# The second normalisation of a mixture-of-experts trunk: its passes shared among VectorE, ScalarE and GpSimd

## The chip, the core and the metric
One core of a Trainium2 chip runs the whole program. The metric is the device time of one execution in microseconds (us); lower is better. The core has five instruction streams that matter here: TensorE (PE), VectorE (DVE), ScalarE (ACT), GpSimd (POOL) and SyncE (SP), which issues transfers. They meet only through semaphores: an instruction increments one when it is done, and another engine waits for a count.

## The reference, cut to what matters
The program is one step of a trunk with 1088 tokens (1024 of a prompt, 64 of a running stream) of 1024 features. The last thing it computes is the second layer normalisation, on all tokens:

```python
def layer_norm(x, g, b):
    mu = jnp.mean(xf, -1, keepdims=True)
    var = jnp.mean(jnp.square(xf - mu), -1, keepdims=True)
    return ((xf - mu) * lax.rsqrt(var + LN_EPS) * g + b)
...
    x = layer_norm(ALPHA * x + jnp.einsum('bte,ed->btd', merged, w_out), ln1_g, ln1_b)   # h2
    ffn = routed_experts(h2, idx, wts, w_eg, w_eu, w_ed) + shared
    x = layer_norm(ALPHA * x + ffn, ln2_g, ln2_b)        # the second normalisation
```

Everything is float32. The reference has ahead of it a mixer (stick-breaking attention and a recurrence) and a router with 64 experts, of which each token uses 8.

## The kernel before, in words
`build` runs the mixer, a bridge (first normalisation, router, shared expert), the loop over 64 experts, `overflow` (skipped at run time when no expert overflows), and last `combine`, which holds the second normalisation. Only `combine` is touched. Each part is a `Phase`: a block of instructions for each engine with its own semaphores, and a barrier of all engines at its end, so nothing of `combine` starts before the experts are through.

The expert loop's sums lie in device memory (`ys_d`). The residual rows `xr`, the gain `gcol` and the shift `bcol` (the last two the same on all 128 partitions) were loaded to SBUF near the end of the expert loop (L2047 to L2049). `combine` works on nine tiles `t` of 128 tokens by 1024 features; the last has 64 tokens (`rows(t)`). SP issues all nine loads of `ys` at once (L2485), then, for each tile in order, waits for `y_ready` and stores the tile (L2490). For each tile the engines do this:

- DVE, `add` (L2498): y = ALPHA * xr + y, one pass over 1024 columns, with the row sum as accumulator.
- ACT: the mean from the sum (L2528, one column), then (y - mean) squared with its row sum (L2530, one pass), then the root of the variance (L2532, one column).
- DVE, `finish`: z = (y - mean) * gain (L2505, one pass, written over `xr`), the reciprocal of the root (L2508, one column), and y = z * reciprocal + shift (L2511, one pass).

DVE's written order is `add(0)`, `add(1)`, `finish(0)`, `add(2)`, `finish(1)` and so on to `finish(8)`: an `add` runs one tile ahead. The order is written out by hand; an engine does its instructions strictly in that order, and waits at the first whose semaphore isn't there. GpSimd has no instruction in `combine`. PE has none either.

`scalar_tensor_tensor` takes two tensors and one value for each partition: (in0 op0 scalar) op1 in1. In all three passes of DVE both tensors lie in SBUF.

Of the kernel before, what the change touches and what calls it, by code (L numbers as in the profile page):

```python
# [16 lines left out]
ACT = mybir.ActivationFunctionType  # L17
ALU = mybir.AluOpType
# [7 lines left out]
NT = (T + P - 1) // P  # L26
# [32 lines left out]
def rows(t):  # L59
    return P if t < NT - 1 else T - P * (NT - 1)  # L60
# [79 lines left out]
def build(nc, a, o):  # L140

    ctx = ExitStack()
    with ctx:
# [61 lines left out]
        overflow(nc, a, ps, ident, h2_d, ys_d, tok_d, plan_d, gates_d, only_d, dest_d, picks_d, pairs_d, step_d, limit_d, bufs)  # L205
        c2.close()
        combine(nc, o, ys_d, *ahead)


# [2256 lines left out]
def combine(nc, o, ys_d, gcol, bcol, xr):  # L2466


    with ExitStack() as c:
        ys = c.enter_context(nc.sbuf_tensor("ysr", [P, NT, D], F32))  # L2470
        total, mean, spread, root, inverse = (c.enter_context(nc.sbuf_tensor(n, [P, NT], F32))
                                              for n in ("total2", "mean2", "spread2", "root2", "inverse2"))
        sq = c.enter_context(nc.sbuf_tensor("sq2", [P, 2, D], F32))
        eps = c.enter_context(nc.sbuf_tensor("eps2", [P, 1], F32))
        with Phase(nc, "x_in0 x_in1 x_in2 x_in3 x_in4 x_in5 x_in6 x_in7 x_in8 eps_set summed centre spread_ready root_ready inverted "
                       "gained y_ready stored") as (block, (
                x_in0, x_in1, x_in2, x_in3, x_in4, x_in5, x_in6, x_in7, x_in8, eps_set, summed, centre, spread_ready, root_ready,
                inverted, gained, y_ready, stored)):
            x_in = (x_in0, x_in1, x_in2, x_in3, x_in4, x_in5, x_in6, x_in7, x_in8)

            @block.sync  # L2481
            def _(sp):
                for t in range(NT):
                    m = rows(t)
                    sp.dma_start(ys[:m, t, :], ys_d[t * P:t * P + m, :]).then_inc(x_in[t], 16)  # L2485
                for t in range(NT):
                    m = rows(t)
                    sp.wait_ge(y_ready, t + 1)
                    dst = o[0][0, t * P:t * P + m, :] if t < NT - 1 else o[1][0, :, :]
                    sp.dma_start(dst, ys[:m, t, :]).then_inc(stored, 16)  # L2490
                sp.wait_ge(stored, 16 * NT)

            @block.vector
            def _(dve):
                def add(t):
                    m = rows(t)
                    dve.wait_ge(x_in[t], 16)
                    dve.scalar_tensor_tensor(out=ys[:m, t, :], in0=xr[:m, t, :], scalar=ALPHA, in1=ys[:m, t, :], op0=ALU.mult, op1=ALU.add,  # L2498
                                             accum_out=total[:m, t:t + 1]).then_inc(summed, 1)

                def finish(t):
                    m = rows(t)
                    y, z = ys[:m, t, :], xr[:m, t, :]
                    dve.wait_ge(centre, t + 1)
                    dve.scalar_tensor_tensor(out=z, in0=y, scalar=mean[:m, t:t + 1], in1=gcol[:m, :], op0=ALU.add,  # L2505
                                             op1=ALU.mult).then_inc(gained, 1)
                    dve.wait_ge(root_ready, t + 1)
                    dve.reciprocal(inverse[:m, t:t + 1], root[:m, t:t + 1]).then_inc(inverted, 1)  # L2508
                    dve.wait_ge(inverted, t + 1)
                    dve.wait_ge(gained, t + 1)  # L2510
                    dve.scalar_tensor_tensor(out=y, in0=z, scalar=inverse[:m, t:t + 1], in1=bcol[:m, :], op0=ALU.mult,  # L2511
                                             op1=ALU.add).then_inc(y_ready, 1)

                dve.memset(eps[:, :], LN_EPS).then_inc(eps_set, 1)
                for t in range(NT):
                    add(t)
                    if t >= 1:
                        finish(t - 1)
                finish(NT - 1)

            @block.scalar
            def _(act):
                act.wait_ge(eps_set, 1)
                for t in range(NT):
                    m = rows(t)
                    col = slice(t, t + 1)
                    act.wait_ge(summed, t + 1)
                    act.activation(mean[:m, col], total[:m, col], ACT.Copy, scale=-1.0 / D).then_inc(centre, 1)  # L2528
                    act.wait_ge(centre, t + 1)
                    act.activation(sq[:m, t % 2, :], ys[:m, t, :], ACT.Square, bias=mean[:m, col], accum_out=spread[:m, col]).then_inc(spread_ready, 1)  # L2530
                    act.wait_ge(spread_ready, t + 1)
                    act.activation(root[:m, col], spread[:m, col], ACT.Sqrt, scale=1.0 / D, bias=eps[:m, :]).then_inc(root_ready, 1)  # L2532

# [25 lines left out]
```

## Time and profile before

| | |
|---|---|
| time, median of 3 runs | 2656.3 us (2650.55 to 2661.9) |
| the profiled execution | 2651.97 us, span 2650.3 us |
| busy over the span | PE 92%, PEld 82%, DVE 73%, ACT 52%, POOL 51% |
| `combine`, 2607.0 to 2650.3 us | 43.3 us, of which DVE busy 33.5, ACT 16.8, POOL 0 and PE 0 |

A row of the timeline gives an instruction's start in us from the span's start, its duration in us, its engine and line, its operation, what it writes and reads with partitions x elements, and in square brackets the time that the engine sat idle before it and what ended that. A duration counts from the point where the engine takes the instruction up: an instruction that is taken up and then held shows a long duration, not an idle time. A run of instructions on one engine overlaps by some hundredths of a us, so the distance from start to start is a little less than the duration. A row of the groups gives line, engine, operation, names, shapes and count, then busy us in total, mean ns of one, and the idle time before them.

### The profile page before, as it was taken

The page shows a single profiled execution, that of the slowest core. Times are in us where ns is not written, and L with a number is a line of the kernel's source. Part 1 is how long each engine was busy: PE and PEld are TensorE (multiplying, and loading weights), DVE is VectorE, ACT ScalarE, POOL GpSimd, SP SyncE. Part 2 cuts the span into 40 slices and gives each one's busy share as a digit, 9 for nine tenths or more (in the row PEclk, how much of TensorE's full clock was granted, in tenths as well). Part 3 has the DMA queues.
Part 4 walks back from the last instruction along what each step waited for, and adds up shares of the span by engine and source line. Part 5 has one row for each costly group of instructions (what it writes and reads, how often), then busy time and mean ns, then how long its engine had stood idle before and what let it go on. Part 6 is the DMA issues. An engine that isn't in the chain of part 4 may idle for free. (4 is left out here: it accounts for less than half of the span.)

```text
span 2650.3 us, 40161 instructions
## 1 busy us (share of the span) xinstructions
PE 2431.2 (92%) x14824; PEld 2183.7 (82%) x14824; DVE 1923.1 (73%) x3073; ACT 1373.6 (52%) x2032; POOL 1339.5 (51%) x1317
## 2 busy tenths in 40 slices
PE   4999999999999999999986999699999999999990
PEld 4889898898998989989875775499989898888980
DVE  7475765757758567575676687578888888888875
ACT  3443625426245263452633332267777777777772
POOL 6354664646546556455564265334555455554320
PEclk9999999999999999999987999799999999999995
DMA  5201111111110111101113323489999999999994
GB/s 183 61 26 33 54 34 45 34 40 46 42 45 28 39 45 39 57 25 41 45 73 115 102 75 134 119 261 285 311 305 310 302 303 311 307 313 313 352 333 162
DMA packets 207582, 380.77 MB, mean 144 GB/s; under 512 B 22694, under 2 KB 129546, under 8 KB 206874
## 3 DMA queue, kind: packets, MB, share of 16 engines
q1 hardware_dynamic: 180330, 302.31, 33.0%
q0 software_dynamic: 25824, 71.42, 11.8%
q10 hardware_dynamic: 1232, 4.46, 0.4%
q8 instruction: 119, 1.95, 0.3%
q14 instruction: 77, 0.63, 0.1%
HBM read 314.84 MB, written 72.97 MB: 146 GB/s over the span
## 5 line engine op out<-in xcount | busy, mean ns | idle before, releaser
L122 PE MATMUL ps<-xTh,w_mix_low 128*128 128x368 f32 (+1 forms) x1728 | 595.8, 345 | 10.2 <-POOL w_mix_low L116 8.8
L123 PE MATMUL ps<-xTl,w_mix_high 128*128 128x368 f32 (+1 forms) x1728 | 569.6, 330 | 0.0
L124 PE MATMUL ps<-xTh,w_mix_high 128*128 128x368 f32 (+1 forms) x1728 | 567.5, 328 | 0.0
L2087 POOL DMA_INDIRECT ys_d<-yo,tab_early x114 | 214.2, 1879 | 426.9 <-DVE yo L2259 263.9
L122 PEld LDWEIGHTS ps<-xTh,w_mix_low 128*128 128x128 f32 x1728 | 326.0, 189 | 21.9 <-issue 18.6
L123 PEld LDWEIGHTS ps<-xTl,w_mix_high 128*128 128x128 f32 x1728 | 326.2, 189 | 9.1 <-issue 6.2
L124 PEld LDWEIGHTS ps<-xTh,w_mix_high 128*128 128x128 f32 x1728 | 325.6, 188 | 0.0
L2129 PE MATMUL ps<-xghl,wgh 128*128 128x320 f32 (+5 forms) x1024 | 271.4, 347 | 13.5 <-DVE xghl L116 6.9
L2129 PE MATMUL ps<-xghl,wuh 128*128 128x320 f32 (+5 forms) x1024 | 263.4, 344 | 0.0
L2131 PE MATMUL ps<-xghl,wgl 128*128 128x160 f32 (+5 forms) x1024 | 240.0, 234 | 0.0
L2131 PE MATMUL ps<-xghl,wul 128*128 128x160 f32 (+5 forms) x1024 | 238.6, 233 | 0.0
L1275 POOL TENSOR_TENSOR x_m<-x_m,kh_m 128x128 f32<-128x128 f32 (+1 forms) x272 | 126.8, 466 | 218.0 <-ACT x_m L828 218.0
L116 POOL TENSOR_TENSOR w_mix_low<-w_mix_raw,w_mix_high 128x1024 fp32r<-128x1024 f32 x72 | 174.6, 2426 | 88.5 <-ACT w_mix_high L111 88.2
L2129 PEld LDWEIGHTS ps<-xghl,wgh 128*128 128x128 f32 x1024 | 194.3, 190 | 28.6 <-ACT yo L2201 13.8
L2131 PEld LDWEIGHTS ps<-xghl,wgl 128*128 128x128 f32 x1024 | 198.0, 193 | 1.2
L2131 PEld LDWEIGHTS ps<-xghl,wul 128*128 128x128 f32 x1024 | 196.3, 192 | 0.0
L116 DVE TENSOR_TENSOR wdl<-wd_early,wdh 128x2048 fp32r<-128x2048 f32 x64 | 146.8, 2294 | 64.4 <-ACT wdh L111 64.4
L2129 PEld LDWEIGHTS ps<-xghl,wuh 128*128 128x128 f32 x1024 | 192.4, 188 | 0.0
L2075 POOL DMA_INDIRECT xg_early<-h_d,tab_early x72 | 168.9, 2346 | 42.2 <-issue 21.4
L116 DVE TENSOR_TENSOR wul<-wu_early,wuh 128x2048 fp32r<-128x2048 f32 x64 | 146.7, 2292 | 37.7 <-ACT wuh L111 37.7
L1255 POOL CAST sph_m<-l_m 128x128 fp32r<-128x128 f32 (+3 forms) x112 | 60.0, 536 | 203.1 <-PE ps L596 142.2
L2201 ACT ACTIVATE yo<-ps,wcol 128x512 f32<-128x512 f32 x228 | 143.9, 680 | 10.7 <-issue 5.3
(378 smaller groups left out, 5968.8 us busy)
## 6 DMA issues: line engine op xcount, KB each, us to landing
wd_early<-in_w_exp_down SPq DMA_DIRECT2D x64, 1024.0 KB, 9.2
wg_early<-in_w_exp_gate SPq DMA_DIRECT2D x124, 512.0 KB, 7.5
wu_early<-in_w_exp_up SPq DMA_DIRECT2D x124, 512.0 KB, 5.8
w_mix_raw<-in_w_in SPq DMA_DIRECT2D x72, 512.0 KB, 3.9
mT_d<-gs_m SPq DMA_DIRECT2D x8, 544.0 KB, 2.7
xr_m<-in_x_prompt SPq DMA_DIRECT2D x8, 512.0 KB, 3.7
xn_d<-xr_m SPq DMA_DIRECT2D x8, 512.0 KB, 2.8
out<-vrow_m SPq DMA_DIRECT2D x8, 512.0 KB, 4.8
```

Source lines behind the costliest of these rows:

```text
L116: return dve.tensor_tensor(lo, x, hi.bitcast(F32), ALU.subtract)
L122: pe.matmul(out, ll, rh, start=start, stop=False)
L123: pe.matmul(out, lh, rl, start=False, stop=False)
L124: return pe.matmul(out, lh, rh, start=False, stop=stop)
L1255: pool.tensor_copy(high, l[:kr, s, 0:wd]).then_inc(hi_done, 1)
L1275: pool.tensor_tensor(xs, xs, seg(q, LEVELS[i], side), ALU.mult).then_inc(x_done, 1)
L2075: pool.indirect_dma_start(out=xg[:m, b, j, :], out_offset=None, in_=h2_d[:, :], in_offset=rows_of(e, j, m), bounds_check=last_row, oob_is_ ...
L2087: pool.indirect_dma_start(out=ys_d[:, :], out_offset=rows_of(e, j, m), in_=yo[:m, b, j, :], in_offset=None, compute_op=ALU.add, bounds_che ...
L2129: pe.matmul(ps[:, bank + f, 0:2 * cap], wh[:, k, cols], xhl[:, k, 0:2 * cap], start=k == 0, stop=False, skip_group_check=True)
L2131: mm = pe.matmul(ps[:, bank + f, 0:cap], wl[:, k, cols], xhl[:, k, 0:cap], start=False, stop=k == KT - 1, skip_group_check=True)
L2201: act.activation(yo[:m, b, j, q * 512:(q + 1) * 512], ps[part, DB[n], :], ACT.Copy, scale=wcol[part, b, j:j + 1]).then_inc(y_ready, 1)
```

## The change
It touches `combine` alone.

- ACT gets a pass more: it writes xr = y - mean (`Identity` with the mean as bias, signalled by the new semaphore `centred`), and then squares that instead of y - mean.
- DVE's `finish` becomes `scale`: the reciprocal, and one pass, y = xr * reciprocal * gain. The centring pass is gone from it. `scale` runs two tiles behind `add`, not one.
- GpSimd gets a pass: y = y + shift, after which the tile is signalled as ready for its store.

```diff
-                def finish(t):
+                def scale(t):
                     m = rows(t)
-                    y, z = ys[:m, t, :], xr[:m, t, :]
-                    dve.wait_ge(centre, t + 1)
-                    dve.scalar_tensor_tensor(out=z, in0=y, scalar=mean[:m, t:t + 1], in1=gcol[:m, :], op0=ALU.add,
-                                             op1=ALU.mult).then_inc(gained, 1)
                     dve.wait_ge(root_ready, t + 1)
                     dve.reciprocal(inverse[:m, t:t + 1], root[:m, t:t + 1]).then_inc(inverted, 1)
                     dve.wait_ge(inverted, t + 1)
-                    dve.wait_ge(gained, t + 1)
-                    dve.scalar_tensor_tensor(out=y, in0=z, scalar=inverse[:m, t:t + 1], in1=bcol[:m, :], op0=ALU.mult,
-                                             op1=ALU.add).then_inc(y_ready, 1)
+                    dve.wait_ge(centred, t + 1)
+                    dve.scalar_tensor_tensor(out=ys[:m, t, :], in0=xr[:m, t, :], scalar=inverse[:m, t:t + 1], in1=gcol[:m, :],
+                                             op0=ALU.mult, op1=ALU.mult).then_inc(gained, 1)
...
                 for t in range(NT):
                     add(t)
-                    if t >= 1:
-                        finish(t - 1)
-                finish(NT - 1)
+                    if t >= 2:
+                        scale(t - 2)
+                scale(NT - 2)
+                scale(NT - 1)
+
+            @block.gpsimd
+            def _(pool):
+                for t in range(NT):
+                    m = rows(t)
+                    pool.wait_ge(gained, t + 1)
+                    pool.tensor_tensor(ys[:m, t, :], ys[:m, t, :], bcol[:m, :], ALU.add).then_inc(y_ready, 1)
...
                     act.wait_ge(centre, t + 1)
-                    act.activation(sq[:m, t % 2, :], ys[:m, t, :], ACT.Square, bias=mean[:m, col], accum_out=spread[:m, col]).then_inc(spread_ready, 1)
+                    act.activation(xr[:m, t, :], ys[:m, t, :], ACT.Identity, bias=mean[:m, col]).then_inc(centred, 1)
+                    act.wait_ge(centred, t + 1)
+                    act.activation(sq[:m, t % 2, :], xr[:m, t, :], ACT.Square, accum_out=spread[:m, col]).then_inc(spread_ready, 1)
```

## Rows read from the trace of the kernel before
**Rows 1.** Busy time by stage: us, then each engine's busy us and count, clock, DMA share, GB/s.

```profile
2607.00:2650.30 43.30, 0.00 (x0) 0.00 (x0) 33.51 (x46) 16.81 (x37) 0.00 (x0) 0.50 0.55 206
```

**Rows 2.** The chain that ended last, parts of it: start us, us, what.

```profile
2618.67 1.20 DVE xr L2505
2619.87 0.09 DVE inverse L2508
...
2619.98 1.28 DVE ysr L2511
2621.26 1.14 DVE ysr L2498 x2
2622.40 1.20 DVE xr L2505
...
2644.97 1.28 DVE ysr L2511
```

**Rows 3.** Timeline of SP: the last store of the program.

```profile
2646.27 0.51 SPq L2490 DMA_DIRECT2D out<-ysr  x1
```

**Rows 4.** Timeline of ACT and DVE at the first tiles of `combine`.

```profile
2612.26 0.20 ACT L2528 ACTIVATE mean<-total 128x1 f32<-128x1 f32 x1 [19.84 <-DVE ysr L2498]
2612.50 1.15 ACT L2530 ACTIVATE sq<-ysr,mean 128x1024 f32<-128x1024 f32 x1
...
2613.76 1.28 ACT L2532 ACT_TABLE_LOAD   x1
...
2615.05 0.29 ACT L2532 ACTIVATE root<-spread,eps 128x1 f32<-128x1 f32 x1
2615.25 0.19 ACT L2528 ACTIVATE mean<-total 128x1 f32<-128x1 f32 x1
...
2616.04 0.15 DVE L2508 RECIPROCAL inverse<-root 128x1 f32<-128x1 f32 x1
2616.24 1.28 DVE L2511 SCALAR_TENSOR_TENSOR ysr<-xr,inverse,bcol 128x1024 f32<-128x1024 f32 x1
```

**Rows 5.** ScalarE's lines L887 (Identity) and L883 (Sqrt), alternating: min/median/max ns.

```profile
L887 ACT ACTIVATE xr_m<-xr_m,st x9: 1240/1242/1247, 9.3 to 53.8; 128x1024 f32<-128x1024 f32 x8, 64x1024 f32<-64x1024 f32 x1
...
L883 ACT ACT_TABLE_LOAD  x1: 1283/1283/1283, 3.1 to 3.1; - x1
```

**Rows 6.** GpSimd's timeline near the start: two-input passes over 1024 columns.

```profile
21.02 2.34 POOL L116 TENSOR_TENSOR w_mix_low<-w_mix_raw,w_mix_high 128x1024 fp32r<-128x1024 f32 x1
23.31 3.32 POOL L1311 TENSOR_TENSOR xr_m<-xr_m,b_in_m 128x1024 f32<-128x1024 f32 x1
```

**Rows 7.** GpSimd's timeline at the end of the bridge.

```profile
1595.52 0.97 POOL L1902 DMA_INDIRECT tok_d<-pairs,dest  x1 [0.30 <-issue]
1614.66 2.34 POOL L1894 TENSOR_TENSOR y<-y,bcol 64x1024 f32<-64x1024 f32 x1 [18.17 <-DVE y L1632]
```

**Rows 8.** VectorE's timeline in the stretch of rows 6, and a little later.

```profile
21.20 3.23 DVE L1157 TENSOR_TENSOR xr_m<-xr_m,g_in_m 128x1024 f32<-128x1024 f32 x1
...
24.55 2.10 DVE L1149 SCALAR_TENSOR_TENSOR st<-st 128x1 f32<-128x1 f32 x1
...
33.61 0.16 DVE L1149 SCALAR_TENSOR_TENSOR st<-st 128x1 f32<-128x1 f32 x1
...
36.94 1.22 DVE L1157 TENSOR_TENSOR xr_m<-xr_m,g_in_m 128x1024 f32<-128x1024 f32 x1
```

**Rows 9.** Timelines near 191 us: GpSimd, and a VectorE pass that reads PSUM.

```profile
191.17 2.34 POOL L116 TENSOR_TENSOR w_mix_low<-w_mix_raw,w_mix_high 128x1024 fp32r<-128x1024 f32 x1
...
191.95 1.23 DVE L1088 TENSOR_TENSOR pm_m<-ps,masks 128x1024 f32<-128x1024 f32 x1 [1.24 <-PE ps L654]
```

**Rows 10.** The load of tile 2, issued at 2607.9: count, KB, us to landing.

```profile
ysr<-ys_d SPq DMA_DIRECT2D x1, 512.0 KB, 7.1
```

**Rows 11.** Timelines near 1461 us: VectorE's pass, then GpSimd's that waited for it.

```profile
1460.24 1.23 DVE L1632 TENSOR_TENSOR y<-y,gcol 128x1024 f32<-128x1024 f32 x1
...
1461.64 2.36 POOL L1894 TENSOR_TENSOR y<-y,bcol 128x1024 f32<-128x1024 f32 x1 [13.06 <-DVE y L1632]
```

More of the change, by code:

```diff
@@ L2475, in combine @@
         with Phase(nc, "x_in0 x_in1 x_in2 x_in3 x_in4 x_in5 x_in6 x_in7 x_in8 eps_set summed centre spread_ready root_ready inverted "
-                       "gained y_ready stored") as (block, (
+                       "gained y_ready stored centred") as (block, (
                 x_in0, x_in1, x_in2, x_in3, x_in4, x_in5, x_in6, x_in7, x_in8, eps_set, summed, centre, spread_ready, root_ready,
-                inverted, gained, y_ready, stored)):
+                inverted, gained, y_ready, stored, centred)):
             x_in = (x_in0, x_in1, x_in2, x_in3, x_in4, x_in5, x_in6, x_in7, x_in8)
```

## The prediction
> **What bounds the kernel now.** I looked first for where the touched code stands in the span. The table of busy time by stage shows the last 43.3 us of a span of 2650.3 as a stage by itself: PE and GpSimd do nothing in it, DVE is busy for 33.5 us and ACT for 16.8 [rows 1]. All that comes before is untouched and ends in a barrier, so the change can only move these 43.3 us, 1.6% of the program. The shares of the whole page (PE 92%) say nothing here.
>
> Then the chain that ended last. Once the first loads are in, it never leaves DVE: 1.14 for the add, 1.20 for the centring, 0.11 for the reciprocal and the wait behind it (2619.87 to 2619.98), 1.28 for the last pass, then the next tile [rows 2]. From one centring to the next it is 2622.40 - 2618.67 = 3.73 us a tile, with ACT's work and the stores beside it. The last pass starts at 2644.97 and ends at 2646.25; SP issues its store at 2646.27 [rows 3], and the span ends 4.05 us after that pass. So DVE bounds the stage now, at three passes a tile.
>
> **The change part by part.** *DVE.* The centring pass goes: 9 x 1.20 = 10.8 us off DVE's own work. What stays for a tile is add 1.14 + reciprocal and wait 0.11 + scale 1.20 = 2.45 us; the product takes the place of a sum in the last pass, at the same shape and with the same two SBUF tensors, so I give it the same duration.
>
> *ACT.* For a tile it now has the mean 0.24 (2612.26 to 2612.50), the centring, the squares with their accumulator 1.26 (2612.50 to 2613.76) and the root 0.20 to 0.31 (2615.05 to the next mean at 2615.25, or to its own end and a wait) [rows 4]. The added pass isn't in this stage's trace. The nearest rows are the squares with a bias, 1.15, and the Identity passes of the first normalisation, which have a scale too, 1.24 [rows 5]; they are its two ends, and I take 1.15, since the new pass has a bias alone, and 0.04 for the wait behind it: 1.19. ACT comes to 3.0 us a tile, still under 3.73. The wait for `centred` inside ACT holds only the squares of the same tile.
>
> *GpSimd.* Nine two-input passes over 1024 columns. The trace has this very form: 2.34 alone, also for 64 partitions [rows 6, 7], from start to start 2.29 (21.02 to 23.31). I count 2.31 between neighbours.
>
> If the three engines worked side by side, ACT would bound the stage at 3.0. But the trace shows that GpSimd's pass and a DVE pass on two SBUF tensors do not overlap. At 21.20 DVE takes up a product of two SBUF tensors while GpSimd is in a pass from 21.02 to 23.36; the product takes 3.23 us and ends at 24.43, where the same line takes 1.22 undisturbed [rows 6, 8]. It stood still until 23.2 and then ran in full. GpSimd's next pass is taken up at 23.31, while DVE's has the way, and lasts 3.32 instead of 2.34: it in turn began at 24.3, as DVE ended. DVE's `scalar_tensor_tensor` on a single column, 0.16 us elsewhere, then takes 2.10 and ends at 26.65, with GpSimd's end at 26.63 [rows 6, 8]. And a DVE pass that takes one tensor from PSUM ran 1.23 us in the middle of a GpSimd pass of 2.34, both undisturbed [rows 9]. So the pair is exclusive, for whole instructions and in both directions, when DVE reads two tensors from SBUF; `add` and `scale` both do.
>
> The Trainium skill says the same in SBUF — State Buffer, "SBUF: two separate sides": VectorE and GpSimd share a port pair under an exclusive lock, which a two-SBUF-input instruction of VectorE needs against a GpSimd one that reads SBUF, and the loser blocks for the whole instruction. Its next section, "A bandwidth-pool intuition that's wrong (but worth ruling out)", says of one such case that the loser goes on about 115 ns after the winner's end. The rows above show no such gap: by that figure, an estimate, the 14 handovers counted below would bring 1.6 us over the sum without gaps.
>
> So the exclusive work of a tile becomes add 1.14 + GpSimd 2.31 + scale 1.20 = 4.65 us, in place of 3.73. *The order of it.* GpSimd's pass t waits for `scale(t)`; when that ends, DVE's next `add` has been waiting in line and goes first. Then DVE does a reciprocal and waits for its semaphore, and GpSimd has the way; the next `scale` is held until it is through, and behind `scale` in DVE's line stand the `add` of a later tile and so ACT's mean of it. ACT has two to three tiles of lead, so this costs no more than the lock itself.
>
> *The start.* The loads are as before. `scale(0)` needs `root(0)`: before it ended at 2615.34, now 1.19 later, 2616.53; the reciprocal and its wait take 0.20 (2616.04 to 2616.24) [rows 4], so `scale(0)` starts at 2616.75. Ahead of it in DVE's line stands `add(2)`, whose load was issued at about 2607.8 and landed 7.1 us later, 2614.9 [rows 10]: done by 2616.1, hidden. The table load of 1.28 ahead of the first root stays [rows 4].
>
> *The sum.* From 2616.75: `scale(0)` 1.20; six rounds of `add`, GpSimd, `scale` (adds 3 to 8), 6 x 4.65 = 27.9; then there is no `add` left, and GpSimd 6, `scale(7)`, GpSimd 7, `scale(8)`, GpSimd 8 follow one another, where GpSimd starts each time 0.17 us after DVE's signal, as it did behind DVE's pass of 1460.24 to 1461.47 [rows 11]: 3 x 2.31 + 3 x 0.17 + 2 x 1.20 + 0.03 = 9.9. With `scale(0)` that is 39.0, and ends at 2655.7, against 2646.25 before: +9.5 us. The observed pair was a little tighter: from 21.02 to 26.63, GpSimd, DVE and GpSimd took 5.61 where pitches of 2.31, 1.15 and 2.35 give 5.81, 0.1 less for each handover. With 14 of them (two in each round, two in the tail) the sum falls by 1.4, to +8.1. I take +8.5, nearer to the pair that was seen. The tail behind the last pass stays at 4.05 us: the store is the same, and stores come 4.5 us apart instead of 3.7.
>
> The profiled execution took 2651.97, so the changed one should take 2660.5. The median of the runs shown is 4.3 higher, 2656.3; I set the prediction on it: 2656.3 + 8.5 = 2664.8.
>
> **The rivals.** (1) *The engines overlap*, because what was seen at 21 us has another cause, or GpSimd's adds fall into DVE's gaps. Then ACT bounds the stage: `root(0)` at 2616.53, eight more tiles at 3.0 us, `root(8)` at 2640.5; then 0.2 + 1.28 for `scale(8)`, 0.17 + 2.34 for the shift, ending at 2644.5, 1.8 us before the 2646.25 of now. Time 2654.5. It is the one case that is not slower. It decides from the point where DVE is held for less than 3.73 - 2.45 = 1.28 us of GpSimd's 2.31 in a tile. For it speaks that the exclusion was read in one stretch alone, and that a GpSimd pass and a DVE pass do overlap where one operand is in PSUM [rows 9]; against it speak all three waits of rows 6 and 8.
>
> (2) *ACT swaps tables for every tile*, if Identity and Sqrt don't stand in one. Two loads of 1.28 would make ACT 5.6 us a tile: eight tiles 44.8 behind 2616.53, then 1.5, 2.5 and 4.05: span 2669.4, +19 us, 2675.4. Against it: in the first normalisation Identity and Sqrt alternate nine times behind a single load [rows 5].
>
> (3) *GpSimd's first pass comes late*, since all it did for the last thousand us was to issue indirect transfers. In the bridge its two-input pass came behind a series of these and took 2.34 with no delay other than its wait for DVE [rows 7]. The Trainium skill (GPSIMD Engine Reference, "2.1 Instruction dispatch") gives some 6 us for the first call of freshly loaded code, which does not show in the profile. Worked out from rows, as a late start of one whole GpSimd pass and its round, 4.65 us behind `scale(0)`, the time would be 2669.5, as the lock would stand idle meanwhile.
>
> **How the numbers follow.** The forecast (alternation under the lock) gets 85%, rival 1 8%, rival 2 2%, rival 3 3%, and 2% are left for what I don't see. The forecast's own bounds are +8.1 and +9.5, with ACT's 1.24 instead of 1.15 lost behind the lock; more comes from the spread of the executions, 2650.55 to 2661.9, which moves a median of a few runs by 3 to 4 us. The range is 2656 to 2671: it holds nearly all of the forecast and rival 3, and leaves out most of rivals 1 and 2. Half a per cent, about what a measurement of this kernel can tell from no change, is 13.3 us. The forecast's 8.5 lies inside it, so most of its 85% is "same"; a share of some 14% of it, by the spread, and rivals 2 and 3 in part make "slower" 0.17; faster by so much would need a third of the stage to vanish, 0.02.
>
> **What would show it.** Right: in `combine`, DVE's `scale` passes with durations near 3.3 us (1.2 + most of 2.3) and no idle time named for them, GpSimd's passes near 3.4 where an `add` is ahead of them, one tile every 4.5 to 4.65 us, ACT idle for a third of the time, and the last GpSimd pass 4 us before the end. DVE's busy time in the stage would rise although it lost a pass. Wrong: `scale` at 1.28 and a tile every 3.0 us (rival 1), more than one table load (rival 2), or a gap between the first `scale` and the first GpSimd pass (rival 3). The forecast fails as a number if stages ahead of 2607 move too.

## The result and the profile after
The changed kernel takes 2663.02 us (median of 15 runs, 2656.51 to 2668.04) against 2653.81 us of the kernel before (15 runs, 2648.97 to 2661.9): ratio 1.0033, 95% interval 1.0025 to 1.0041. It is slower by 9 us, clear of the noise and under half a per cent. The profiled execution took 2660.16 us, span 2658.4.

Where the time went, by busy time in the stage (us, then busy us and count of PE, PEld, DVE, ACT, POOL, the clock, DMA share and GB/s), to set against [rows 1]:

```profile
2607.00:2658.40 51.40, 0.00 (x0) 0.00 (x0) 38.33 (x37) 26.03 (x46) 26.59 (x9) 0.50 0.46 174
```

The stage is 8.1 us longer. VectorE was relieved of nine passes of 1.2 us, and its busy time rose from 33.5 to 38.3. The timeline of one round in the steady part shows why (start us, us, engine, line, operation, what is written and read, in brackets idle time before it and its releaser):

```profile
2627.18 1.21 DVE L2498 SCALAR_TENSOR_TENSOR ysr<-xr,ysr 128x1024 f32<-128x1024 f32 x1
2627.34 3.26 POOL L2523 TENSOR_TENSOR ysr<-ysr,bcol 128x1024 f32<-128x1024 f32 x1 [1.16 <-DVE ysr L2507]
...
2628.32 0.15 DVE L2504 RECIPROCAL inverse<-root 128x1 f32<-128x1 f32 x1
...
2628.51 3.18 DVE L2507 SCALAR_TENSOR_TENSOR ysr<-xr,inverse,gcol 128x1024 f32<-128x1024 f32 x1
...
2631.03 0.29 ACT L2538 ACTIVATE root<-spread,eps 128x1 f32<-128x1 f32 x1
2631.61 1.21 DVE L2498 SCALAR_TENSOR_TENSOR ysr<-xr,ysr 128x1024 f32<-128x1024 f32 x1
...
2641.79 3.18 DVE L2507 SCALAR_TENSOR_TENSOR ysr<-xr,inverse,gcol 128x1024 f32<-128x1024 f32 x1
...
2645.05 2.34 POOL L2523 TENSOR_TENSOR ysr<-ysr,bcol 128x1024 f32<-128x1024 f32 x1 [1.16 <-DVE ysr L2507]
...
2652.04 2.33 POOL L2523 TENSOR_TENSOR ysr<-ysr,bcol 64x1024 f32<-64x1024 f32 x1 [1.16 <-DVE ysr L2507]
```

Read it from the ends. GpSimd's pass ends at 2630.60 (2627.34 + 3.26), the scale at 2631.69, 1.09 later. Undisturbed, the scale takes 1.28 us and GpSimd's pass 2.34, so of the scale, taken up at 2628.51, only the last 1.28 us were work, from 2630.41; and of GpSimd's pass, taken up at 2627.34, only the last 2.34, from 2628.26, as the add ended (2628.39). Nothing in brackets stands before the scale: a pass that is held is busy, not idle. From add to add it is 4.43 us, where [rows 2] have 3.73. ACT has the root ready and waits. The last three rows are the tail: with no add ahead, GpSimd's passes show their own 2.34.

The groups by line and shape (count, then busy us, mean ns of one, idle time before them) say the same in total:

```profile
L2523 POOL TENSOR_TENSOR ysr<-ysr,bcol 128x1024 f32<-128x1024 f32 x8 | 24.3, 3032 | 32.0 <-DVE ysr L2507 32.0
L2507 DVE SCALAR_TENSOR_TENSOR ysr<-xr,inverse,gcol 128x1024 f32<-128x1024 f32 x8 | 23.5, 2935 | 0.3
...
L2534 ACT ACTIVATE xr<-ysr,mean 128x1024 f32<-128x1024 f32 x8 | 9.2, 1150 | 0.3
L2536 ACT ACTIVATE sq<-xr 128x1024 f32<-128x1024 f32 x8 | 8.5, 1058 | 0.3
...
L2538 ACT ACT_TABLE_LOAD x1 | 1.3, 1283 | 0.0
```

And the chain that ended last (start us, us, what) shows how a held pass looks in that view: since no semaphore ends the hold, the pass of 3.18 us stands there almost whole, hold and work together, as 3.06 us of "issue" a tile.

```profile
2627.18 1.22 DVE ysr L2498 x2
2628.40 0.09 DVE inverse L2504
...
2628.51 0.04 DVE ysr L2507
2628.55 3.06 issue
2631.61 1.22 DVE ysr L2498 x2
```

### The profile page after: what moved, and what is told of

Same layout as the page of the kernel before. It is cut to its first block and busy times, and to the rows that moved or that the text cites. A ratio compares the mean times of both kernels' runs of the same rounds, so it can differ in the third digit from the quotient of the medians.

```text
span 2658.4 us, 40170 instructions
## 1 busy us (share of the span) xinstructions
PE 2432.0 (91%) x14824; PEld 2184.1 (82%) x14824; DVE 1927.8 (73%) x3064; ACT 1382.8 (52%) x2041; POOL 1375.7 (52%) x1326
## 5 line engine op out<-in xcount | busy, mean ns | idle before, releaser
L2087 POOL DMA_INDIRECT ys_d<-yo,tab_early x114 | 221.8, 1946 | 416.0 <-DVE yo L2259 267.3
L2129 PEld LDWEIGHTS ps<-xghl,wgh 128*128 128x128 f32 x1024 | 194.8, 190 | 29.3 <-ACT yo L2201 14.6
L116 DVE TENSOR_TENSOR wgl<-wg_early,wgh 128x2048 fp32r<-128x2048 f32 x64 | 146.2, 2285 | 3.7 <-ACT wgh L111 3.7
```

The costliest lines, as they stand in the source:

```text
L116: return dve.tensor_tensor(lo, x, hi.bitcast(F32), ALU.subtract)
L2087: pool.indirect_dma_start(out=ys_d[:, :], out_offset=rows_of(e, j, m), in_=yo[:m, b, j, :], in_offset=None, compute_op=ALU.add, bounds_che ...
L2129: pe.matmul(ps[:, bank + f, 0:2 * cap], wh[:, k, cols], xhl[:, k, 0:2 * cap], start=k == 0, stop=False, skip_group_check=True)
```

## The experiments
Executions differ much ahead of the stage: its first add starts anywhere from 2610.3 to 2629.7 us in the profiled executions below. So beside the time I give the stage's own length, from the start of the first add to the end of the last pass: 35.3 us in the kernel before (2610.93 to 2646.25), 43.0 in the changed one (2611.38 to 2654.37). Each such length is of one profiled execution.

The theory is that of the prediction: a GpSimd pass and a VectorE pass on two SBUF tensors exclude each other, so their times add. Its main rival is that the chain of hand-overs among three engines costs the time.

**The shift back on VectorE.** GpSimd has nothing to do; the rest of the change stays.

```diff
-                    pool.tensor_tensor(ys[:m, t, :], ys[:m, t, :], bcol[:m, :], ALU.add).then_inc(y_ready, 1)
+                    dve.wait_ge(gained, t + 1)
+                    dve.tensor_tensor(ys[:m, t, :], ys[:m, t, :], bcol[:m, :], ALU.add).then_inc(y_ready, 1)
```

> The changed kernel with the shift taken from GpSimd and given to VectorE as a third pass (a product and a sum of two SBUF tensors); ScalarE still centres. Theory (the exclusive pair): with GpSimd out, no VectorE pass is held. VectorE's work in a tile is add 1.15 + reciprocal 0.11 + scale 1.20 + shift 1.2 = 3.7 us, ScalarE's 2.8; the scale passes show 1.28 us, not 3.2, a tile takes 3.7, and the whole is within 1 us of the kernel before (ratio 0.9995 to 1.0007). Rival (the long chain of hand-overs between three engines is what costs, and the added wait for ScalarE's centring is part of it): the scale passes stand behind named idle time, a tile takes over 4 us, and half or more of the +9 us stays (ratio above 1.0017).

2655.41 us against 2653.52 of the kernel before, ratio 1.0009, 0.9997 to 1.0021. The timeline of VectorE:

```profile
2626.90 1.28 DVE L2507 SCALAR_TENSOR_TENSOR ysr<-xr,inverse,gcol 128x1024 f32<-128x1024 f32 x1
...
2628.22 1.22 DVE L2510 TENSOR_TENSOR ysr<-ysr,bcol 128x1024 f32<-128x1024 f32 x1
2629.36 1.22 DVE L2498 SCALAR_TENSOR_TENSOR ysr<-xr,ysr 128x1024 f32<-128x1024 f32 x1
...
2630.69 1.28 DVE L2507 SCALAR_TENSOR_TENSOR ysr<-xr,inverse,gcol 128x1024 f32<-128x1024 f32 x1
```

The scale is at 1.28, a tile takes 3.79 (a little over the 3.7, since the shift waits for the scale's signal), the stage 36.3. Of the 7.7 us by which the stage grew, 6.7 hang on where the shift is done; ScalarE's centring, the wait for it and the two tiles of lead bring 1.0 together.

**No shift at all.** GpSimd's block left out, `scale` signals `y_ready`; the output lacks the shift.

> The changed kernel without the shift: GpSimd's pass is left out and nothing takes its place, so the output lacks the shift. Theory (exclusive pair): all that GpSimd's pass brought goes, VectorE has 2.45 us of work in a tile and ScalarE 2.79 (2616.79 to 2619.57 between two means in the changed kernel), so ScalarE bounds: last root near 2639.2, last scale pass ends near 2640.7, span near 2645, 5.5 us under the kernel before (ratio near 0.998) and 13.5 under the changed one, i.e. more than 9 x 1.2. Rival (ScalarE's added pass, or its writes over xr, slow the chain too): a tile takes over 3 us and the gain on the kernel before is under 3 us.

2646.88 us against 2653.52, ratio 0.9982, 0.9968 to 0.9995; stage 29.3 us (2611.81 to 2641.10), 6.0 under the kernel before and 13.7 under the changed one. ScalarE bounds it, from root to root 2.79:

```profile
2628.16 0.29 ACT L2531 ACTIVATE root<-spread,eps 128x1 f32<-128x1 f32 x1
2628.49 0.16 DVE L2504 RECIPROCAL inverse<-root 128x1 f32<-128x1 f32 x1 [0.16 <-ACT root L2531]
...
2630.95 0.29 ACT L2531 ACTIVATE root<-spread,eps 128x1 f32<-128x1 f32 x1
```

This is what the change would have reached in its steady part had GpSimd's pass been free. The pass costs 13.7 us for nine: on average 1.5 a tile over what ScalarE asks.

**The gain in PSUM.** ScalarE copies it there once, while the stage waits for its loads; the scale then reads one tensor from SBUF and one from PSUM. Same passes, same engines, same order.

```diff
+            gain = ps[:, 0:2, :].rearrange("p b n -> p (b n)")
...
-                    dve.scalar_tensor_tensor(out=ys[:m, t, :], in0=xr[:m, t, :], scalar=inverse[:m, t:t + 1], in1=gcol[:m, :],
+                    dve.scalar_tensor_tensor(out=ys[:m, t, :], in0=xr[:m, t, :], scalar=inverse[:m, t:t + 1], in1=gain[:m, :],
...
+                act.activation(gain, gcol[:, :], ACT.Copy).then_inc(gain_in, 1)
```

> The changed kernel with the gain copied once to PSUM by ScalarE at the stage's start; the scale pass reads xr from SBUF and the gain from PSUM. The same passes on the same engines, in the same order. Theory (the pair is exclusive only where VectorE reads two tensors from SBUF): the scale passes show about 1.3 us beside a GpSimd pass, only add and GpSimd alternate, a tile takes 1.1 + 2.2 = 3.3 us, the last GpSimd pass ends near 2645.1 and the span near 2649.2: 9 us under the changed kernel, 1 us under the kernel before (ratio 0.9990 to 1.0000). Rival A (GpSimd's pass excludes any VectorE pass): scale passes near 3.2 us, a tile takes 4.43 us and the time is the changed kernel's, ratio 1.003. Rival B (two reads share a bandwidth): scale passes between 1.5 and 2.5 us, a tile near 4.

2652.68 us against 2653.52, ratio 0.9994, 0.9983 to 1.0006; stage 33.9, 9.1 under the changed kernel. The timeline:

```profile
2624.01 9.94 POOL L2526 TENSOR_TENSOR ysr<-ysr,bcol 128x1024 f32<-128x1024 f32 x3
2625.24 1.28 DVE L2510 SCALAR_TENSOR_TENSOR ysr<-xr,inverse,ps 128x1024 f32<-128x1024 f32 x1
...
2626.44 1.98 DVE L2499 SCALAR_TENSOR_TENSOR ysr<-xr,ysr 128x1024 f32<-128x1024 f32 x1
...
2628.54 1.28 DVE L2510 SCALAR_TENSOR_TENSOR ysr<-xr,inverse,ps 128x1024 f32<-128x1024 f32 x1
```

GpSimd does three passes without a gap beside it, 3.3 us each, its own 2.3 and the wait for an add. The scale is never held; the add, which still reads two SBUF tensors, now is (1.98 in place of 1.22). From scale to scale 3.30 us, as expected from add and GpSimd alone. This settles the theory against the hand-overs, of which there are as many as in the changed kernel, and against rivals A and B of the expectation.

**The last shift on VectorE as well.** 

> As the kernel with the gain in PSUM, but the last tile's shift is done by VectorE and not by GpSimd. Theory: the last tile's shift takes 1.2 us behind GpSimd's eighth pass in place of 2.3, so it ends 1.1 us earlier: span near 2648.1, 2 us under the kernel before (ratio 0.9985 to 0.9997). Rival (a VectorE wait for GpSimd's signal costs as much as the pass saves): the same as with the gain in PSUM.

2651.6 us, ratio 0.9994, 0.9982 to 1.0006; stage 32.9, 1.0 less, where 1.1 was expected. The times can't tell it from the one before; the stage, of one execution each, can. The last pass waits for GpSimd's eighth and is then done in 1.22:

```profile
2646.65 1.22 DVE L2515 TENSOR_TENSOR ysr<-ysr,bcol 64x1024 f32<-64x1024 f32 x1 [2.36 <-POOL ysr L2530]
```

**GpSimd's pass twice.** The output has the shift once too often. 

> The changed kernel with GpSimd adding the shift twice (the output has it once too often), the second pass behind the first. Theory (exclusive, nothing of GpSimd hidden): every further pass costs its full 2.2 us, a tile takes 4.43 + 2.2 = 6.65, the time is about 20 us over the changed kernel. Rival (part of the 4.43 is waiting of the hand-overs, in which a second GpSimd pass fits): less than 1.5 us a tile, under 14 us in all.

One execution: 2679.63 us; stage 62.5, 19.5 over the changed kernel. A tile takes 6.57 us, so the further pass costs 2.14 of its 2.34, and now the add is held too:

```profile
2644.61 3.33 POOL L2523 TENSOR_TENSOR ysr<-ysr,bcol 128x1024 f32<-128x1024 f32 x1
...
2645.85 3.17 DVE L2507 SCALAR_TENSOR_TENSOR ysr<-xr,inverse,gcol 128x1024 f32<-128x1024 f32 x1
2648.01 3.20 POOL L2525 TENSOR_TENSOR ysr<-ysr,bcol 128x1024 f32<-128x1024 f32 x1
...
2648.94 3.35 DVE L2498 SCALAR_TENSOR_TENSOR ysr<-xr,ysr 64x1024 f32<-64x1024 f32 x1
2651.18 3.33 POOL L2523 TENSOR_TENSOR ysr<-ysr,bcol 128x1024 f32<-128x1024 f32 x1
```

So the 4.43 us of a tile hold at most 0.2 us into which GpSimd's work would fit.

**A one-input scale on VectorE.**

```diff
-                    dve.scalar_tensor_tensor(out=ys[:m, t, :], in0=xr[:m, t, :], scalar=inverse[:m, t:t + 1], in1=gcol[:m, :],
-                                             op0=ALU.mult, op1=ALU.mult).then_inc(gained, 1)
+                    dve.tensor_scalar(ys[:m, t, :], xr[:m, t, :], inverse[:m, t:t + 1], None, ALU.mult).then_inc(gained, 1)
```

> The changed kernel with VectorE's scale pass as a product with the reciprocal alone: one SBUF input, no gain (left out). In the first normalisation this form takes 0.81 us for 1024 columns, where two-input ones take 1.22. Theory A (only two tensor inputs from SBUF exclude): the pass shows 0.81 beside GpSimd's, add and GpSimd alternate and a tile takes 3.3. Theory B (the fast one-input form needs GpSimd's way too): the pass is held for GpSimd's length, shows about 2.7 us, and a tile takes 1.1 + 2.2 + 0.75 = 4.05.

One execution: 2673.68 us, of which some 18 us lie ahead of the stage (its first add starts at 2629.71), in code that is the same; the time is no evidence. The stage takes 38.2, a tile 3.89 to 3.90:

```profile
2635.45 0.75 DVE L2507 TENSOR_SCALAR ysr<-xr,inverse 128x1024 f32<-128x1024 f32 x1
...
2645.25 2.64 DVE L2507 TENSOR_SCALAR ysr<-xr,inverse 128x1024 f32<-128x1024 f32 x1
...
2647.81 1.21 DVE L2498 SCALAR_TENSOR_TENSOR ysr<-xr,ysr 128x1024 f32<-128x1024 f32 x1
```

0.75 us with GpSimd idle, 2.64 with GpSimd at work: theory B. So "two tensors from SBUF", which the prediction took as the condition, is not the whole of it: the fast form with one input is held as well. What ran beside GpSimd's pass without being held is the scale with a PSUM operand, and the one-column reciprocal (0.15 throughout); that a pass is small isn't enough, since the one-column pass on two SBUF tensors of [rows 8] took 2.10.

**A one-input pass on GpSimd.**

```diff
-                    pool.tensor_tensor(ys[:m, t, :], ys[:m, t, :], bcol[:m, :], ALU.add).then_inc(y_ready, 1)
+                    pool.tensor_scalar(ys[:m, t, :], ys[:m, t, :], 1.0, None, ALU.add).then_inc(y_ready, 1)
```

> The changed kernel with GpSimd adding a constant in place of the shift: a pass that reads one SBUF tensor, not two (the output's shift is wrong by that). Theory (exclusion for the whole length of any GpSimd pass that reads SBUF): scale passes are held for the length of GpSimd's pass; if that is 1.1 us they show some 2.1, if it is over 2.3 they show 3.2 or more; a tile takes 2.2 us plus GpSimd's length, or ScalarE's 2.79 if that is more. Rival (only a GpSimd pass on two inputs excludes): scale passes at 1.28.

One execution: 2652.24 us, stage 35.2. Here both sides of the expectation missed. GpSimd's line by minimum, median and maximum ns, and then its timeline and VectorE's:

```profile
L2523 POOL TENSOR_SCALAR ysr<-ysr x9: 2761/3139/3692, 2618.5 to 2643.8; 128x1024 f32<-128x1024 f32 x8, 64x1024 f32<-64x1024 f32 x1
```

```profile
2622.13 6.22 POOL L2523 TENSOR_SCALAR ysr<-ysr 128x1024 f32<-128x1024 f32 x2
...
2624.51 1.21 DVE L2498 SCALAR_TENSOR_TENSOR ysr<-xr,ysr 128x1024 f32<-128x1024 f32 x1
...
2625.66 0.15 DVE L2504 RECIPROCAL inverse<-root 128x1 f32<-128x1 f32 x1
2625.84 1.86 DVE L2507 SCALAR_TENSOR_TENSOR ysr<-xr,inverse,gcol 128x1024 f32<-128x1024 f32 x1
2627.62 1.21 DVE L2498 SCALAR_TENSOR_TENSOR ysr<-xr,ysr 128x1024 f32<-128x1024 f32 x1
```

The pass is longer than the shift, 2.76 us undisturbed, and yet a tile takes only 3.11 (2624.51 to 2627.62), and the scale is held 0.58 instead of 1.9. Were the whole pass exclusive, a tile would take 2.76 + 2.2 = 5.0. The exclusive part is at most 3.11 - 2.2 = 0.9 us and at least the 0.58 of the hold, a fifth to a third of it. The end of the stage shows that the rest of the pass does not exclude. The last scale, on two SBUF tensors, runs its 1.28 us inside a GpSimd pass (VectorE's timeline, and GpSimd's of 2638.5 to 2640.9 alone):

```profile
2637.13 1.28 DVE L2507 SCALAR_TENSOR_TENSOR ysr<-xr,inverse,gcol 128x1024 f32<-128x1024 f32 x1
2637.65 3.40 POOL L2523 TENSOR_SCALAR ysr<-ysr 128x1024 f32<-128x1024 f32 x1
...
2639.34 1.28 DVE L2507 SCALAR_TENSOR_TENSOR ysr<-xr,inverse,gcol 64x1024 f32<-64x1024 f32 x1
```

GpSimd's pass is held while the scale of 2637.13 runs (3.40 in place of 2.76), works from about 2638.3 to 2641.05, and does not hold the scale that is taken up 1 us into that. (That scale has 64 rows of the 128, which doesn't spare it: the same one is held in the changed kernel, 3.39 us.) So what excludes lies in the first microsecond of the pass. For the two-input pass the exclusive part is nearly all (2.2 of 2.34). The Trainium skill (SBUF — State Buffer, "SBUF: two separate sides") says that whichever of the two starts first has the shared ports for the whole instruction; the two-input pass agrees to within 0.2 us, this one-input pass does not. Why the exclusive part is so much shorter here, 0.9 at most against 2.2, stays open.

**A GpSimd pass that reads nothing.** A memset of a scratch tile in its place; the shift is left out. (Each memset waits for the one before.)

> The changed kernel with GpSimd's pass replaced by a memset of a scratch tile of the same size, which reads nothing; the shift is left out. VectorE's passes are as in the changed kernel, on two SBUF tensors. Theory A (what excludes is GpSimd's reading of SBUF): nothing is held, the scale passes show 1.28 us, and ScalarE bounds the stage at 2.79 a tile, as without a shift. Theory B (any GpSimd instruction on SBUF excludes a VectorE pass on two SBUF tensors): the memset of some 0.9 us is held behind the add and holds the scale pass; GpSimd's records are near 2 us. The stage stays near ScalarE's 2.79 either way, so the durations tell, not the time.

One execution: 2647.61 us. Theory A: neither side notices the other, though they overlap in each tile.

```profile
2629.59 1.22 DVE L2499 SCALAR_TENSOR_TENSOR ysr<-xr,ysr 128x1024 f32<-128x1024 f32 x1
2629.74 0.95 POOL L2526 MEMSET scratch<- 128x1024 f32 x1 [1.84 <-DVE ysr L2508]
...
2631.18 1.29 DVE L2508 SCALAR_TENSOR_TENSOR ysr<-xr,inverse,gcol 128x1024 f32<-128x1024 f32 x1
```

It shows overlap with the add; the scale starts after the memset has ended (2630.69), so it isn't tested against it.

**One tile of lead in place of two.** 

> The changed kernel with scale one tile behind add, as finish was before, not two. Theory: in the steady part nothing changes, 4.43 us a tile, since root(t) is ready 2.9 us after add(t) and scale(t) comes to its turn 4.4 after it; at the start scale(0) does not stand behind add(2), and an add has its turn later; the stage ends within 1 us of the changed kernel's. Rival (the second tile of lead is needed to hide ScalarE's longer work): a tile takes 5 us or more, the stage over 4 us longer.

One execution: 2668.45 us, with the first add at 2618.77; the stage takes 43.9, 0.95 over the changed kernel, and a tile 4.43. The second tile of lead is worth that 1 us at the start (the first scale starts 5.73 us after the first add either way, waiting for `root(0)`, and the add of tile 2 fills part of that wait) and nothing later.

**Three tiles of lead, with the gain in PSUM and the last shift on VectorE.**

```diff
-                    if t >= 2:
-                        scale(t - 2)
+                    if t >= 3:
+                        scale(t - 3)
+                scale(NT - 3)
                 scale(NT - 2)
                 scale(NT - 1)
```

> The gain in PSUM, the last tile's shift on VectorE, and scale three tiles behind add. Theory: one more add is done before GpSimd's first pass, where it holds nobody, so the steady part has one round less of add against GpSimd: the stage from the first add to the end of the last pass takes 1.1 us less than with two tiles of lead (32.9), 31.8, against 35.3 in the kernel before: ratio near 0.9985. Rival: the fourth load comes so late (about 5.3 us after the first add) that scale(0) waits behind its add and the gain is lost: 32.5 to 33.5.

2650.91 us against 2653.51, ratio 0.9987, 0.9976 to 0.9998; stage 31.9 (2612.90 to 2644.79), 3.4 under the kernel before and 1.0 under two tiles of lead, where 1.1 was expected. The fourth add still fits ahead of the first scale:

```profile
2617.29 1.23 DVE L2499 SCALAR_TENSOR_TENSOR ysr<-xr,ysr 128x1024 f32<-128x1024 f32 x1
2618.11 0.29 ACT L2547 ACTIVATE root<-spread,eps 128x1 f32<-128x1 f32 x1
2618.52 0.16 DVE L2507 RECIPROCAL inverse<-root 128x1 f32<-128x1 f32 x1
2618.71 1.28 DVE L2510 SCALAR_TENSOR_TENSOR ysr<-xr,inverse,ps 128x1024 f32<-128x1024 f32 x1
```

This version leaves nothing out. It is clearly faster than the changed kernel, and faster than the one before by 2.6 us in the medians; the interval of that ratio only just leaves out 1, so the 3.4 us of the stage, from one execution each, is what backs it.

## Why the prediction was right
The forecast was 2664.8 us, +8.5 us; measured are 2663.02 and a ratio of 1.0033, which on 2653.8 is 8.8 us (6.6 to 10.9). Point by point:

- *The stage and its bound.* Only the stage moved: its first add starts at 2611.38 in place of 2610.93.
- *The exclusive pair.* Held, by the gain in PSUM (scale 3.18 to 1.28, stage 9.1 us shorter) and the doubled pass (+2.14 us a tile). Its condition was too narrow on VectorE's side (the fast one-input pass is held too) and too wide on GpSimd's (a pass with one input excludes for 0.9 us at most, not "for whole instructions"). For this change neither makes a difference, since all its long passes on both engines read two SBUF tensors.
- *The rounds.* 4.43 us measured, 4.65 in the sum without handovers, 4.45 with the 0.1 us a handover that was taken from [rows 6, 8]. The small sample was the better guide. The delay of about 115 ns behind the winner, which the Trainium skill (SBUF — State Buffer, "A bandwidth-pool intuition that's wrong (but worth ruling out)") gives for another pair of operations, does not appear: the scale's own 1.28 us begin at 2630.41, 0.19 before the winner's record ends.
- *The start.* `scale(0)` 5.82 us after the first add predicted, 5.73 measured (2617.11). The add of tile 2 was hidden, as expected.
- *The tail.* From the end of `scale(6)` to that of GpSimd's last pass, 9.9 us less 0.2 for two handovers were predicted; it took 9.4 (2644.97 to 2654.37). GpSimd starts 0.08 us behind VectorE's signal, not 0.17. Behind the last pass 4.03 us, as before.
- *The sum.* The stage grew by 7.7 us, under even the lower bound of 8.1 (0.1 less at the start, 0.1 in the rounds and 0.3 in the tail, 0.1 more in `scale(0)` itself). The medians differ by 9.2; what that has over 7.7 is within the interval, and no run says where it arises. So the mechanism was right, while the closeness of 8.5 to 8.8 is partly luck: it was chosen between bounds that both lie above what the stage grew by. So is that of 2664.8 to 2663.02, since the base of 2656.3, a median of three, was 2.5 us above that of 15.
- *ScalarE.* Predicted at 3.0 us a tile, measured 2.79: the squares without a bias take 1.06, not 1.15, and the next mean starts 0.20 behind the root, where the sum had the upper of its two values, 0.31. It was hidden in the changed kernel.
- *The marks.* Predicted scale near 3.3 and GpSimd near 3.4, VectorE's busy time up: 3.18, 3.26, and 33.5 to 38.3. A tile took 4.43, just under the 4.5 to 4.65 named, and the last GpSimd pass ended 4.03 us before the end. One table load, so rival 2 fell. GpSimd's first pass was taken up 0.09 us after the first scale, so rival 3 fell. Rival 1 needed a hold under 1.28 us a tile; the hold was 1.9 on VectorE's side.

## What to carry to other kernels
Work moved from VectorE to GpSimd is only moved if the two can run together. With GpSimd's pass reading two tensors from SBUF they couldn't here, whether VectorE's pass had two SBUF tensors or the fast one-input form, and a further such pass a tile cost 2.14 of its 2.34 us. Before sharing out passes, look in the trace for one that takes longer than its like while GpSimd is at work, and read it by its end, not its start. If a constant operand can stand in PSUM, that pass runs beside GpSimd's (the add, still on two SBUF tensors, does not). That alone brought the same division of work, 9 us too slow, back to the time before; with a longer lead and a shorter tail as well it was 2.6 us faster in the medians, 0.5 to 6.4 by the interval.

## What the runs showed that I had not expected
- A VectorE pass with one SBUF input and a value for each partition, 0.75 us alone, takes 2.64 beside GpSimd's two-input pass.
- A GpSimd pass that adds a constant takes 2.76 us for 1024 columns, more than adding a tensor (2.34), and excludes VectorE for at most the first 0.9 us or so of it.
- A GpSimd memset (0.95 us) and an add on two SBUF tensors overlap with no hold on either side, as one of the two theories had it.
- Where both wait, VectorE's held pass goes ahead of GpSimd's next: with the gain in PSUM the add got its turn between each two GpSimd passes that stood in line without a gap, so neither engine was starved. It had also been taken up first each time, so these runs don't tell a preference for VectorE from first come, first served.
